# Attention pipeline: the mixing product and its copy-out come one step earlier

## What is computed

```python
s = jnp.einsum('bqhgd,bshd->bhgqs', qn, kn).astype(jnp.float32) + bias
s = jnp.where(mask, s, NEG_INF)
p = jax.nn.softmax(s, axis=-1)        # with sinks: e / (sum(e) + exp(sink - m))
out = jnp.einsum('bhgqs,bshd->bqhgd', p.astype(vn.dtype), vn)
```

## Time and profile before

| | |
|---|---|
| median of 3 runs | 2075.28 us (2071.97 to 2080.11) |
| profiled execution, its own time | 2080.11 us |
| span of its trace | 2078.3 us |
| TensorE busy (matmul) | 2003.3 us, 96% of the span |
| VectorE, ScalarE, GpSimd busy | 1053.4, 786.9, 299.5 us |
| first call of `attention` | about 684 to 767 us from the start of the span |
| second call | about 877 to 938 us |
| third call | about 1500 to 1645 us |

### The profile page before, as it was taken

How to read it: one execution, slowest core, us unless ns; L and a number is a source line. 1 busy time by engine, 2 the same in 40 slices (tenths; PEclk the granted TensorE clock), 3 DMA queues, 4 the chain that set the end, 5 groups by cost and what they waited for, 6 DMA issues and landing times. The chain is left out here.

```text
span 2078.3 us, 25188 instructions
## 1 busy us (share of the span) xinstructions
PE 2003.3 (96%) x9682; PEld 1531.5 (74%) x9682; DVE 1053.4 (51%) x1974; ACT 786.9 (38%) x1391; POOL 299.5 (14%) x392
## 2 busy tenths in 40 slices
PE   7999999999999999899999999998799999999998
PEld 5787778887657567667788888876666678888886
DVE  5467544434569655385544443343366654444322
ACT  3343434423333563374332222224277642232322
POOL 2450000010000641051000000001055310000000
PEclk9999999999999999999999999999699999999999
DMA  7452324343322222213333333355000133333331
GB/s 172 134 162 71 102 82 150 131 145 92 82 61 71 61 52 82 81 32 92 99 93 92 94 94 94 94 128 176 16 2 2 42 88 95 100 93 92 94 92 69
DMA packets 316749, 187.14 MB, mean 90 GB/s; under 512 B 33487, under 2 KB 297167, under 8 KB 316374
## 3 DMA queue, kind: packets, MB, share of 16 engines
q1 hardware_dynamic: 310222, 168.62, 29.0%
q10 hardware_dynamic: 6408, 16.91, 2.1%
HBM read 183.27 MB, written 17.96 MB: 97 GB/s over the span
## 5 line engine op out<-in xcount | busy, mean ns | idle before, releaser
L251 PE MATMUL banks<-xs,wlo 128*128 128x512 f32 x1336 | 540.6, 405 | 5.0 <-PEq L1456 2.8
L252 PE MATMUL banks<-xs,whi 128*128 128x512 f32 x1336 | 530.5, 397 | 0.0
L253 PE MATMUL banks<-xs,whi 128*128 128x512 f32 x1336 | 530.3, 397 | 0.0
L1611 DVE TENSOR_TENSOR wlo<-raw,whi 128x1024 fp32r<-128x1024 f32 (+1 forms) x283 | 359.3, 1271 | 310.8 <-ACT whi L1602 310.4
L1602 ACT ACTIVATE whi<-raw 128x1024 fp32r<-128x1024 f32 (+1 forms) x283 | 293.6, 1039 | 248.4 <-PE banks L253 183.8
L251 PEld LDWEIGHTS banks<-xs,wlo 128*128 128x128 f32 x1336 | 252.5, 189 | 75.5 <-issue 13.1
L252 PEld LDWEIGHTS banks<-xs,whi 128*128 128x128 f32 x1336 | 252.5, 189 | 62.6 <-issue 3.3
L253 PEld LDWEIGHTS banks<-xs,whi 128*128 128x128 f32 x1336 | 252.4, 189 | 61.2
L2139 ACT ACTIVATE prob<-prob,stat 128x384 f32<-128x384 f32 (+5 forms) x256 | 136.2, 533 | 78.9 <-DVE stat L2062 78.3
L413 POOL TENSOR_TENSOR squares<-squares,x_tmp 128x512 f32<-128x512 f32 x35 | 46.9, 1340 | 749.9 <-ACT x_tmp L405 749.9
L251 PE MATMUL banks<-a_hi,wlo 128*128 128x512 f32 x352 | 139.9, 397 | 0.0
(11 more groups left out here) (335 smaller groups left out, 2785.6 us busy)
## 6 DMA issues: line engine op xcount, KB each, us to landing
raw<-in_ffn_w_gu SPq DMA_DIRECT2D x88, 512.0 KB, 3.8
raw<-in_e_w_in SPq DMA_DIRECT2D x56, 512.0 KB, 3.8
raw<-in_ffn_w_down SPq DMA_DIRECT2D x32, 512.0 KB, 4.0
s_skew<-s_bias ACTq DMA_DIRECT2D x6, 2560.0 KB
raw<-in_o_w_in SPq DMA_DIRECT2D x21, 512.0 KB, 4.0
raw<-in_e_w_out SPq DMA_DIRECT2D x16, 512.0 KB, 3.8
raw<-in_b_w_in SPq DMA_DIRECT2D x15, 512.0 KB, 3.8
raw<-in_ffn_w_down SPq DMA_DIRECT2D x16, 384.0 KB, 3.4
```

The lines of the kernel that those rows point to most:

```text
L251: nc.tensor.matmul(out, k.wlo[:, chunk.slot, at, :], self.x_hi(kt), start=first, stop=False)
L252: nc.tensor.matmul(out, k.whi[:, chunk.slot, at, :], self.x_lo(kt), start=False, stop=False)
L253: ins = nc.tensor.matmul(out, k.whi[:, chunk.slot, at, :], self.x_hi(kt), start=False, stop=last)
L1611: self.nc.vector.tensor_tensor(self.wlo[:, chunk.slot, 0:chunk.blocks, :], self.raw[:, chunk.slot, 0:chunk.blocks, :], hi.bitcast(F32), AL ...
```

## The change

`mix` and `finish` are issued one iteration earlier. `finish(s)` still comes one iteration after `mix(s)`, and nothing else moves. TensorE's iteration s becomes `score(s)`, `turn(s - 3)`, `mix(s - 4)`. VectorE's begins with `finish(s - 5)`. The loops, over `NS + FINISH` iterations, are one iteration shorter.

```diff
         steps = [(m, t, e) for m in range(MT) for e in range(branches) for t in (3, 1, 2, 0)]
         NS = len(steps)
-        TURN, MIX, FINISH = 3, 5, 6
+        TURN, MIX, FINISH = 3, 4, 5
         sg = self.sig
```

## The result

The changed kernel takes 2087.98 us (median of 4 runs, 2087.64 to 2089.24) against 2075.20 us for the kernel before (4 runs on the same chip, 2071.97 to 2080.11). The ratio is 1.0057, with a 95% interval of 1.0041 to 1.0074: slower by 12.8 us. The forecast was 2080.9 us, a loss of 5.6. So the sign was right and the loss 2.3 times as large. The measured ratio lies just over the line of 0.5%, where the forecast had given 0.15; its interval reaches to both sides of that line. Three more executions of the changed kernel, the profiled one among them, took 2085.21, 2085.87 and 2086.27 us; with them the median is 2087.64.

The account below looks back on a forecast made before the run. TensorE was taken as the bound. Terms of 3.6 + 4.4 - 1.5 - 0.9 = +5.6 us on the median of 2075.3 gave 2080.9 us (+0.27%), range 2073 to 2088.

Parts of the forecast that it names:

- TensorE is the bound and its runs keep their price in any order: Attention calls: TensorE is full; the 0.17 us before each run is a price that reordering leaves.
- the rival of closed gaps: Gaps of 0.17 us ahead of mixes were waits a sooner mix could close; half gives 2064 us; chance 0.03.
- The wait for `finish` at t = 3 goes away: First and third call: 0.09 and 0.06 us per group vanish, -1.5 us in all.
- The copy of t = 2 is late, because it stands behind the exponentials of t = 1: ScalarE takes this copy only after two exponentials, so its mix, now an iteration sooner, must wait.
- The rival that no copy is late: Exponential and copy run earlier, so new waits vanish, leaving -2.4 us: 2073 us; chance 0.12.
- The second call: 0.52 for each group: Mix of t = 2 waits 0.52 us for its copy in 7 groups: +3.6 us, group 7.1 us long.
- the lateness is twice as large: Mix of t = 3 waits too in the second call, 0.3 instead of 0.2 elsewhere: 2087 us; chance 0.12.
- The signs of being wrong: No wait for line 2148, that wait at t = 3 too, or a clock below 1.00 in the windows.
- The first and third call: 0.20, with bounds of 0.15 to 0.25: Mix of t = 2 waits 0.20 us for its copy in 22 places: +4.4 us.
- the 0.05 for the semaphore: Time from the copy's end to its mix, taken as 0.05 us from a VectorE logit waiting for a score.
- The ends: -0.9: Starts and ends of the three calls: costlier heads and shorter tails sum to -0.9 us, bounds -3.7 and +2.2.
- The clock falls: New idling could drop TensorE's clock; the second call's 61 us would take 42 more: 2117 us; chance 0.03.

Follow-up runs that it names:

- a second copy: Changed kernel with a useless ScalarE copy of the t = 2 banks to scratch ahead of the real one: 2106.02 us, ratio 1.0150 to the kernel before.
- the same second copy before the change: Kernel before the change with a useless ScalarE copy of the t = 2 banks to scratch ahead of the real one: 2078.62 us, ratio 1.0012.
- the swapped waits: Changed kernel where mix waits first for its copy and then for finish, instead of the other way round: 2085.12 us, ratio 1.0052 to the kernel before.
- the run with the memsets: Changed kernel with eight one-column memsets of scratch put ahead of VectorE's loop in the third call: 2085.04 us in one run.

## Why the prediction was right and where it was short

- *TensorE is the bound and its runs keep their price in any order.* Right. With the copy out of the way the groups are at 8.53, 9.19 and 6.58 us, the old ones less the waits for `finish`. The 0.17 between runs stayed, so the rival of closed gaps falls.
- *The wait for `finish` at t = 3 goes away.* Right, 0.06 and 0.09 in each group.
- *The copy of t = 2 is late, because it stands behind the exponentials of t = 1.* Right, and shown from three sides: taking the exponentials from before it removes the whole loss, a second copy is paid in full, and the same second copy before the change is nearly free. The rival that no copy is late falls.
- *The second call: 0.52 for each group.* 0.59 measured, and 0.12 more for the mix of t = 3, for which the text had allowed 0.03 of margin. The group is 0.71 longer and not 0.5. That second wait was the mechanism of the rival "the lateness is twice as large", at a quarter of its size there. The text also had the logit of t = 1 held by VectorE's own queue and not by TensorE; now it starts 0.05 us after the end of its score (914.08 + 0.70 to 914.83), so it is TensorE's score that holds it, 2.67 after the group's first score instead of 2.57.
- *The signs of being wrong.* One of them was a wait for line 2148 at t = 3. It came: those 0.12 in the second call, too short for the view to name their reason, and 0.65 to 0.68 us once at the end of each call.
- *The first and third call: 0.20, with bounds of 0.15 to 0.25.* 0.36 in the third, outside the bounds. This is the step that failed, as a size. Its terms: score to logit was 0.86 where the text took the middle of 0.75 and 0.85; the 0.05 for the semaphore was 0.14. The 0.05 was read where VectorE waits for TensorE. TensorE's wait for a copy, as the second of two waits, is another case, which no row of before showed, and the swapped waits show that the order makes the difference. It is worth 0.09 in 29 places, 2.6 us. In the second call it also helped to eat the margin of t = 3, where the wait is worth 0.8; the copy of t = 3 ended 0.04 later there than taken as well (1.18 after the group's first score instead of 1.14), and with the waits swapped 0.06 of the 0.12 is left, so the order is only about half of it. The 0.06 at the logit is worth 1.3 in 22 places.
- *Nothing for VectorE's stream.* Its gap of 0.42 every fourth group lands on the new path: 4 x 0.36 = 1.4 us. Before the change it did not show. The first call has one such group: its logit of t = 3 starts 0.36 later than in the others, and the group is 0.2 longer.
- *The ends: -0.9.* Tails: -1.07, -1.11, -1.07, as forecast. Heads, from the first matmul of a call to the score of t = 0 of its second group: +0.9, +0.5, +1.2, and in each of them is one group's new waiting (0.39, 0.71, 0.36), which the forecast had counted under the waits. Without it the heads are worth +1.2 and the ends -2.1, inside the bounds of -3.7 and +2.2. The head of the second call shows no cost, where 0.6 to 1.1 had been taken. But these are single traces, and heads differ between traces of the same instructions: in the run with the memsets, which issues none in the first two calls, their heads are 18.67 and 15.05 us against 19.17 and 14.81. So a head is known to some tenths of a us only.
- *The sum.* By calls, the distances between the scores of t = 0 give +2.0, +4.2, +5.6, the heads +2.6, the tails -3.3: +11.3 in the traces. Sorted as in the forecast it is +13.4 for the waits, where 6.5 was forecast, and -2.1 for the ends, where it was -0.9. Of the 6.9 too little for the waits 2.6 + 0.8 + 1.3 + 1.4 = 6.1 are the terms above, and 0.2 the long group of the first call.
- *The range.* 2087.98 lies 0.02 under its upper end of 2088. The forecast's own terms with their bounds, 1.5 for the waits and 3 for the ends, reach no higher than 2080.9 + 4.5 = 2085.4; the upper end came from the rival with its 2087. Of that rival's two conditions the wait at t = 3 was a quarter of its size, and the 0.3 in the first and third call, for which it named no mechanism, was 0.36 to 0.39. That its time was met is in good part luck.
- *The clock falls.* It did not: 1.00 in the same windows. New idle stretches of up to 0.6 us in each group left TensorE at its upper level, 2.4 GHz. The Trainium skill ("TensorE: Matmul & The Clock Gate", section "A second HAM failure mode: psum-queue depth-cycling") warns of a clock lost to such idling; at this size no run here shows it.

The version with the copy ahead of the exponentials beats both kernels, by 3 us against the one before. Its calls took 81.9, 60.4 and 143.4 us.

## What to carry to other kernels

To shorten a pipeline by a step, ask for each consumer what stands ahead of its producer in that engine's own queue; here moving one copy ahead of two exponentials turned a loss of 12.8 us into a gain of 3. Where a new wait has to be priced and the margin is some tenths of a us, read its price from a place with the same kind of wait on the same engine, at the same position among the waits; a constant from elsewhere was wrong by 0.09 us in 29 places here. A slack that seems unused also covers irregularities that no row of the old profile shows.

## What was not expected of the hardware

- TensorE starts 0.05 us after the end of a ScalarE copy when that is the first of its two waits, and 0.14 when it is the second.
- VectorE stands still for 0.42 us, with no reason in the profile, at a fixed place in its instruction stream every 35.9 us of the third call; eight instructions put ahead of the loop made it vanish from view. 128 of its instructions lie from one to the next, and a transfer of 8 KB of instructions starts 0.61 to 0.89 us after each resumption. The cause was not shown.
- One group of the first call is 9.79 instead of 9.58 us in the changed kernel, and 9.69 instead of 9.49 with swapped waits, always the fourth distance after the start. VectorE's logit of t = 3 starts 0.55 instead of 0.19 us after its score there, and a transfer of 8 KB of instructions on queue 14 starts 0.63 us after it (733.47), as in the third call. The kernels before do not have the late logit in this group.
